# RMS roots at eviction, x loaded first, and two key chunks of layer 1 ahead of the dense feed-forward part, in a two-layer decoder step on one core

## The reference

```
h = RMSNorm(x);  z = h @ w_in              # 2560 columns: B, C, x_conv, x_lru, gate
ya = B * dwconv3(C * x_conv)
yb = RG-LRU(dwconv4(x_lru)) * gelu(gate)   # a scan along the prompt
x += [RMSNorm(ya) | RMSNorm(yb)] @ w_mix_out
k, v = RMSNorm(mem) @ w_k, RMSNorm(mem) @ w_v
x += softmax((RMSNorm(x) @ w_q) k^T / 16) v @ w_o   # samples read k, v from a cache
x += SwiGLU(RMSNorm(x))                    # layer 0: dense, 2816 wide
x += top-2-of-8 MoE SwiGLU(RMSNorm(x))     # layer 1
```

## Time and profile before

| | us |
|---|---|
| runs | 1177.85, 1178.97, 1179.41 |
| median of the runs | 1178.97 |
| profiled execution, device time | 1178.98 |
| its span in the trace | 1177.2 |
| PE busy | 1107.9 (94%) |
| DVE busy | 850.4 (72%) |
| ACT busy | 643.4 (55%) |
| POOL busy | 74.7 (6%) |

### The profile page before, as it was taken

How to read it: one execution, slowest core, us unless ns; L and a number is a source line. 1 busy time by engine, 2 the same in 40 slices (tenths; PEclk the granted TensorE clock), 3 DMA queues, 4 the chain that set the end, 5 groups by cost and what they waited for, 6 DMA issues and landing times.

```text
span 1177.2 us, 21150 instructions
## 1 busy us (share of the span) xinstructions
PE 1107.9 (94%) x8394; PEld 1062.7 (90%) x8394; DVE 850.4 (72%) x1140; ACT 643.4 (55%) x735; POOL 74.7 (6%) x83
## 2 busy tenths in 40 slices
PE   5998999897999999999899988999999999999995
PEld 4998998487999999999799668999999999999995
DVE  4879873257665644778965345989889888989886
ACT  4446451145555433447343136677677767767874
POOL 1012110010000000102211021000000000000000
PEclk8999999998999999999899998999999999999998
DMA  7443546772655654444455783799799879988983
GB/s 275 172 154 134 219 164 260 297 273 84 211 178 178 246 184 143 153 163 158 152 210 215 286 320 116 277 358 362 259 356 359 318 286 354 357 305 304 361 335 128
DMA packets 33846, 284.50 MB, mean 242 GB/s; under 512 B 3888, under 2 KB 3888, under 8 KB 4736
## 3 DMA queue, kind: packets, MB, share of 16 engines
q1 hardware_dynamic: 32832, 278.77, 63.6%
q0 software_dynamic: 960, 4.97, 1.3%
HBM read 278.23 MB, written 5.50 MB: 241 GB/s over the span
## 4 chain that ended last, share of the span: by engine, by line
PE 82%; DVE 9%; ACT 5%; issue 2%; DMA 2%; SPq 0%; DVEq 0%; ACTq 0%
PE ps L1335 23%; PE ps L1336 23%; PE ps L1337 23%; PE ps L1542 2%; PE ps L1576 2%; ACT whi L487 2%; PE ps L1669 2%; DVE rstd L806 2%; DVE wlo L779 1%; PE ps L1562 1%; PE ps L1521 1%; DMA raw<-cache_in_dram 1%; PE ps L1744 1%; DVE hf L821 1%; PE ps L1730 1%
## 5 line engine op out<-in xcount | busy, mean ns | idle before, releaser
L779 DVE TENSOR_TENSOR wlo<-raw,whi 128x1024 fp32r<-128x1024 f32 (+2 forms) x376 | 544.9, 1468 | 158.0 <-ACT whi L487 154.9
L487 ACT ACTIVATE whi<-raw 128x1024 fp32r<-128x1024 f32 (+2 forms) x376 | 462.2, 1239 | 241.6 <-PE ps L1337 203.1
L1335 PE MATMUL ps<-a_hi,whi 128*128 128x264 f32 x1056 | 303.3, 287 | 14.0 <-DVE a_lo L812 8.9
L1336 PE MATMUL ps<-a_lo,whi 128*128 128x264 f32 x1056 | 301.1, 285 | 0.0
L1337 PE MATMUL ps<-a_hi,wlo 128*128 128x264 f32 x1056 | 300.9, 285 | 0.0
L1335 PEld LDWEIGHTS ps<-a_hi,whi 128*128 128x128 f32 x1056 | 200.8, 190 | 16.3 <-issue 10.3
L1336 PEld LDWEIGHTS ps<-a_lo,whi 128*128 128x128 f32 x1056 | 200.8, 190 | 0.1
L1337 PEld LDWEIGHTS ps<-a_hi,wlo 128*128 128x128 f32 x1056 | 199.9, 189 | 0.0
L1335 PE MATMUL ps<-whi,xg_hi 128*128 128x352 f32 x512 | 165.8, 324 | 0.0
L1337 PE MATMUL ps<-whi,xg_lo 128*128 128x352 f32 x512 | 164.9, 322 | 0.0
L1336 PE MATMUL ps<-wlo,xg_hi 128*128 128x352 f32 x512 | 164.3, 321 | 0.0
(11 more groups left out here) (282 smaller groups left out, 1542.5 us busy)
## 6 DMA issues: line engine op xcount, KB each, us to landing
raw<-moe_in_dram SPq DMA_DIRECT2D x100, 1408.0 KB, 7.6
raw<-dense_in_dram SPq DMA_DIRECT2D x60, 1024.0 KB, 4.9
raw<-cache_in_dram SPq DMA_DIRECT2D x24, 1024.0 KB, 6.9
raw<-gu_in_dram SPq DMA_DIRECT2D x22, 1024.0 KB, 4.7
raw<-down_in_dram SPq DMA_DIRECT2D x8, 1408.0 KB, 6.1
spare<-cache_in_dram SPq DMA_DIRECT2D x8, 1024.0 KB, 8.2
v_out<-vt POOLq DMA_DIRECT2D x2, 1024.0 KB, 4.9
k_out<-kt POOLq DMA_DIRECT2D x2, 1024.0 KB, 5.5
```

The costliest lines, as they stand in the source:

```text
L487: act.activation(whi[m % 4][:, 0:w], raw[:, k % RAWS, c:c + w], ACT.Copy).then_inc(hi_done, 1)
L779: dve.tensor_tensor(wlo[m % 4][:, 0:w], raw[:, k % RAWS, c:c + w], whi[m % 4][:, 0:w].bitcast(f32), ALU.subtract).then_inc(lo_done, 1)
L1335: pe.matmul(out, w_hi, m_hi_, start=first, stop=False)
L1336: pe.matmul(out, w_hi, m_lo_, start=False, stop=False)
```

## The change

**Roots at eviction.** Since the root is one number for each column, it may be applied after the product. The operand of the IN, Q, gate/up chunks and of the memory is now x * g without the root: ACT writes `x*g` rounded (`stage_hi`, a copy with a scale), DVE subtracts (`stage_lo`, one instruction for each tile), each tile as soon as its x is ready. The root multiplies at eviction: z, q, k and the down products on DVE by `rstd` or `rstm` as a tensor; the values on ACT, with the root of the memory as a number for each partition (`rcol`, turned by two small matmuls); a gate tile by DVE into `sg` ahead of Silu. The sums for the roots are taken by PE inside the first chunk of the stage that needs them (`folded_sum`, ahead of its last quarter), which for the start and the memory now follow folds by POOL. `norm` and `mem_operand` go. ACT's part of the gate step now reads `sg` in place of PSUM.

**Order of the chunks.** Layer 0 now begins with IN; all its four key chunks (`KX`) stand between V and MIX. Its last two chunks before the gate/up part are the first two key chunks of layer 1 (`K_NEXT`). Layer 1 has IN, V, its other two key chunks, MIX, Q. Nothing stands between MIX and Q or ahead of IN any more.

**Loads.** SP issues the parameters `pk`, the first weight chunk, x in four pieces, two more chunks, half the memory, a chunk, the other half. The first two cache chunks of the attention wait until PE has finished the chunk ahead of MIX.

**The mixer.** The product ya moves from POOL into `lru_input` on DVE. In the V steps both splits of each chunk come as early as they may: `lo(V+2,0)` and `lo(V+2,1)` stand ahead of the scans, and the values are evicted by ACT.

```diff
             sp.dma_start(pk[:], pk_in).then_inc(s_par, 16)
-            load(dense_in[0, 0], 0, 0, DW)
-            sp.dma_start(x[:], x_in).then_inc(s_x, 16)
+            load(dense_in[0], 0, 0, DW)
+            for j in range(4):
+                sp.dma_start(x[:, 2 * j:2 * j + 2], x_in[:, 2 * j:2 * j + 2]).then_inc(s_x[j], 16)
...
+            def stage_hi(name, dst, k):
+                act.activation(dst[:, k], x[:, k], ACT.Copy, scale=stage_gain(name, k)).then_inc(x_h, 1)
...
             act.wait_ge(consts, 4)
             load_table(ACT.Sqrt)
+            hi(0, 0, 0)
+            act.wait_ge(s_par, 16)
             for j in range(4):
-                act.wait_ge(s_mem[j // 2], 16)
-                square(sq[:, 2 * j:2 * j + 2, 0:MEM], memn[:, 2 * j:2 * j + 2])
-            hi(0, 0, 0)
-            hi(0, 0, 1)
-            root("mem", 1.0 / D)
-            norm_hi("m0", lambda k: hf[:, k:k + 2, 0:MEM], m_hi)
-            act.wait_ge(s_x, 16)
+                act.wait_ge(s_x[j], 16)
+                for k in (2 * j, 2 * j + 1):
+                    stage_hi("mix0", a_hi, k)
+                if j == 0:
+                    hi(0, 0, 1)
...
+            def stage_lo(name, src_hi, dst, ks):
+                for k in ks:
+                    dve.wait_ge(x_h, stage_of(name, k + 1))
+                    dve.scalar_tensor_tensor(out=dst[:, k], in0=x[:, k], scalar=stage_gain(name, k),
+                                             in1=src_hi[:, k].bitcast(f32), op0=ALU.mult,
+                                             op1=ALU.subtract).then_inc(x_l, 1)
...
                 def lru_input():
+                    dve.wait_ge(sc_done, l + 1)
+                    dve.tensor_tensor(sc, sc, z[:, ZB:ZB + G], ALU.mult).then_inc(ya_done, 1)
                     dve.wait_ge(gate_a, G * (l + 1))
...
                     chain(dve.tensor_tensor(hs[:, :, SEQ:T], av[:, :, SEQ:T], st_h, ALU.mult))
+                    lo(0, V + 2, 1)
                     chain.wait()
...
+                def scaled_in(j):
+                    return lambda: dve.tensor_tensor(z[:, 2 * j:2 * j + 2, :], banks(IN + j, T), over_pair(rstd), ALU.mult)
...
                 for j in range(4):
-                    step(0, L + MIX + j, lambda: add_x(L + MIX + j, j))
-                keys(3, L + K_C, first=lambda: norm(f"xattn{l}", "g_x", l))
+                    step(0, MIX + j, lambda: add_x(MIX + j, j),
+                         lambda: stage_lo(f"xattn{l}", xq[:, 0], xq[:, 1], (2 * j, 2 * j + 1)))
+                root_reciprocal(f"xattn{l}")
...
                 if l == 0:
-                    norm("ffn0", "g_ffn", 0)
-                    mem_operand(1)
+                    stage_lo("ffn0", a_hi, a_lo, range(KT))
+                    step(0, K_NEXT, lambda: keys(1, 0, K_NEXT))
+                    root_reciprocal("ffn0")
+                    step(0, K_NEXT + 1, lambda: keys(1, 1, K_NEXT + 1))
...
                     def gated(off, j, last=False):
                         k = GU0 + j
+                        dve.wait_ge(pe_done, off * 2 + (2 * k + 1))
+                        dve.tensor_tensor(sg[k % 2][:], ps[:, 2 * (k % 2), 0:T], rstd[:], ALU.mult).then_inc(gate_s, 1)
                         lo(off, k + 2, 0)
...
+            def first_chunk(k, ready, m_h, m_l, w, beside=None):
                 pe.wait_ge(lo_done, 2 * k + 2)
                 if k >= 2:
                     pe.wait_ge(evac, k - 1)
                 for p in range(4):
-                    pe.wait_ge(n_lo, pair_of(name, p + 1))
+                    if beside and p == 3:
+                        beside()
+                    ready(p)
```

More of the change, by code:

```diff
@@ L547, in _, with mem_squares, body, mem_root @@
             for l in range(DEPTH):
[L548 removed]
+                IN, V, KX, MIX, Q, O = places(l)
                 P = pk[:, l, :]
[L551 to L553 removed]
+                root(f"mix{l}", 1.0 / D)
+                def mem_squares(h):
+                    def body():
+                        act.wait_ge(s_mem[h], 16)
+                        for j in (2 * h, 2 * h + 1):
+                            square(sq_m[:, 2 * j:2 * j + 2], memn[:, 2 * j:2 * j + 2])
+                    return body
+                def mem_root():
+                    act.wait_ge(evac, IN + 1)
+                    root("mem", 1.0 / D)
+                    mem_hi(0, range(4, 8))
+                def mem_col():
+                    act.wait_ge(rc_mm, 1)
+                    act.activation(rcol[:], ps[:, 6, 0:4], ACT.Copy).then_inc(rc_cp, 1)
                 def sigmoids(t0):
@@ new lines, in valued, with run @@
+                def valued(j, body=None):
+                    def run():
+                        k = V + j
+                        if body:
+                            body()
+                        act.wait_ge(pe_done, 2 * k + 2)
+                        for t in range(MT):
+                            ins = act.activation(vt[:, t, j * 256:j * 256 + 256], ps[:, 2 * (k % 2) + t, 0:256],
+                                                 ACT.Copy, scale=rcol[:, 2 * t:2 * t + 1])
+                        ins.then_inc(evac, 1)
+                    return run
@@ L849, in _ @@
             lo(0, 0, 0)
+            stage_lo("mix0", a_hi, a_lo, range(0, 2))
             lo(0, 0, 1)
-            dve.wait_ge(n_rt, order["mem"] + 1)
-            chain(dve.reciprocal(rstm[:], rt[:, 0:MEM]))
-            chain.wait()
-            mem_operand(0)
+            stage_lo("mix0", a_hi, a_lo, range(2, KT))
             lo(0, 1, 0)
@@ L1327, in _ @@
                                 hidden_lo(1)
-            norm("fin", "g_fin", 0)
+            root_reciprocal("fin")
+            for k in range(KT):
+                dve.scalar_tensor_tensor(out=hf[:, k], in0=x[:, k], scalar=col(0, "g_fin", k), in1=rstd[:],
+                                         op0=ALU.mult, op1=ALU.mult).then_inc(n_h, 1)
         @block.tensor
@@ L1459, in _ @@
             pe.wait_ge(consts, 4)
-            for j in range(4):
-                sum_pair("mem", sq, j, w=MEM)
             for l in range(DEPTH):
-                L = LAYER0[l]
+                IN, V, KX, MIX, Q, O = places(l)
+                kt = kts[l]
                 by_a = proj(a_hi, a_lo, T)
+                by_q = proj(xq[:, 0], xq[:, 1], T)
                 by_m = proj(m_hi, m_lo, MEM)
@@ L1500, in _ @@
                 gates(2)
                 gates(3)
-                chunks(L + IN + 6, 4, by_a)
-                chunk(0, L + V, values)
-                chunk(0, L + V + 1, values)
-                chunk(0, L + V + 2, beside_v(lambda: group_sum(f"co{l}", xc)))
-                chunk(0, L + V + 3, beside_v(lambda: group_sum(f"lo{l}", ig)))
-                chunk(0, L + K_B, by_m)
-                first_chunk(L + MIX, f"g{l}", a_hi, a_lo, T)
+                chunks(IN + 6, 2, by_a)
+                if l == 0:
+                    pe.wait_ge(gates_act, 2 * G)
+                    pe.wait_ge(rm_done, 1)
+                    for t in range(MT):
+                        last = pe.matmul(ps[:, 6, 2 * t:2 * t + 2], rstm[:, 128 * t:128 * t + 128], ident[:, 0:2],
+                                         start=True, stop=True)
+                    last.then_inc(rc_mm, 1)
@@ L1511, in _ @@
+                chunks(IN + 8, 2, by_a)
+                pe.wait_ge(m_l, KT * (l + 1))
+                for k in range(V, V + 3):
+                    chunk(0, k, values)
+                chunk(0, V + 3, beside_v(lambda: group_sum(f"co{l}", xc)))
+                chunk(0, KX, proj(m_hi, m_lo, MEM, lambda: group_sum(f"lo{l}", ig)))
+                for k in range(KX + 1, MIX):
+                    chunk(0, k, by_m)
+                first_chunk(MIX, group_in(f"g{l}"), a_hi, a_lo, T)
                 for j in range(1, 4):
-                    chunk(0, L + MIX + j, by_a)
```

398 lines of the change are left out of this document (221 added, 177 removed).

## The result

The changed kernel takes 1149.42 us (median of 1148.81 to 1150.01), against 1178.95: a ratio of 0.9751, with an interval of 0.9734 to 0.9768. The forecast was 1143.6 in a range of 1138 to 1152. So the direction and the range held; the gain is 29.5 us where 35.4 were forecast, and the 5.9 us between them are what the experiments had to find.

The account below looks back on a forecast made before the run. PE bounds the kernel, busy 1107.9 of 1177.2 us, so only its idling, half clock behind it and the start can be won. 7.3 + 0.7 + 21.4 + 7.5 - 1.5 = 35.4; 1178.98 - 35.4 = 1143.6 us, range 1138 to 1152.

Parts of the forecast that it names:

- a. The start: Kernel start: first weight chunk lands at 7.6 us, PE begins at 11.9 instead of 19.24; gain 7.3 us (4.1 to 9.0).
- The chain of 4.3 us: Kernel start: ACT's copies and DVE's subtraction between the first weight chunk's landing and PE's first chunk take 4.3 us.
- b. Sums: Norm sums on PE: eight matmuls become three, plus three for the memory and two tiny ones; gain 0.7 us.
- c. Waits: PE's waits for a_lo (8.9), wlo in V (8.0) and at MIX (3.5), and squares (1.0) go: 21.4 us.
- the walk: Step-by-step timing from PE's start of V: third chunk's second split comes at 10.6 us, wanted at 14.
- d. The clock: Four stretches behind PE's long waits ran at 0.51 to 0.56 of full clock; 7.5 us go with the gaps.
- the clock is full elsewhere: Outside the four slow stretches behind long gaps, PE's granted clock was said to be full, 1.00.
- e. What is added: Evictions multiplying by the root cost nothing; added DVE work and tight margins bring 1.5 us of new stalls (0 to 5).
- belong to code whose order stays, and I leave them at what they are: PE's other waits, in attention and MoE, were taken as unchanged.
- DVE did not fall behind: Rival, chance 0.13: layer 0's IN part overruns on DVE, V's splits come late and the gap stays; 1149.3 us, or 1151.1.
- x was not late: Rival, chance 0.07: x's four transfers come serially, last piece in at 21.4 us, delaying the first chunk's end; 1149.7 us.
- The roots did not stall a third chunk: Rival, chance 0.02: the root chain grows from 5.4 to 10.5 us, five stages stall some 3.3 each; 1160 us.
- the gate chunks kept their time: Slower rival, chance 0.02: gate chain exceeds its 8.7 us room, 22 chunks pay; about 1181. Sign: chunks over 5.8 us.

Follow-up runs that it names:

- e6: Changed kernel with the old order of first loads: both memory halves, parameters, first weight chunk, x in four pieces, three more chunks; 1152.48 us.
- e4: Changed kernel with the second split of the third V chunk behind the recurrence again instead of ahead of its scans; 1153.66 us.
- e8: Changed kernel with three V edits undone: ya on POOL, third chunk's second split behind the recurrence, values evicted by DVE; 1160.25 us.
- e2: Changed kernel without key chunks between O and the gate/up part, its root's sum in the first gate/up chunk; roots stay at eviction; 1156.22 us.
- b1: Kernel before the change with an unused 16-byte tile ahead of the large area, moving it by 32 bytes; 1182.58 us.
- e1: Changed kernel with rcol allocated behind the large area, which returns to its old address; 1145.17 us.
- e7: Changed kernel with two edits: rcol behind the large area, and layer 0's first norm sum behind the first chunk; 1145.41 us.
- e10: Changed kernel with rcol behind the area, first sum behind the first chunk, Q's first-chunk splits ahead of tile staging in the third MIX chunk; 1142.48 us.
- e11: Changed kernel once more, unedited; 1149.21 us.
- e3: Changed kernel with the product ya back on POOL, as before the change; 1152.36 us.
- e9: Changed kernel with 32 unused bytes behind rcol, so the large area begins 64 bytes behind its old place; 1145.60 us.

## Why the prediction was right, and where it was off

**a. The start.** The chain of 4.3 us is 4.36. The landing came at 6.41 instead of 7.6, within its bounds: the memory's share was 3.16 (e6) where I had 3.2 and 0.86 of issue; another 2.1 came from something that the sum did not have. The gain is 8.5 instead of 7.3.

**b. Sums.** 3.36 before; now 20.04 - 18.80 = 1.24 us for the first, 1.10 for the memory's and 0.36 for the two small matmuls. Gain 0.66 for 0.7. But the step ended at the matmuls: the fold on POOL ahead of the first sum ended at 18.74, and PE waited 1.33 for it. That is the wait that took the place of the old one.

**c. Waits.** All of the 21.4 us went from where they were. New ones came: 0.34 at the fourth V chunk of layer 1, which the prediction had named as the tight one and priced at 1.6, and 1.27 at Q, which it had not. At Q I had followed the tiles of x, which were in time, and not the second split of the weights, which stands behind their staging on ACT and DVE. V's split came where the walk had it: by this row of DVE it ended 10.4 us after PE's first matmul of V at 79.94, for 10.6 in the walk.

```profile
89.11 1.22 DVE L873 TENSOR_TENSOR wlo<-raw,whi 128x1024 fp32r<-128x1024 f32 x1
```

The cause as told was too narrow. I credited the split's place with 4.7 us; alone it is 1.7 to 2.1 (e4), and the three edits share it (e8). For the gate/up part the prediction named the two key chunks as cover for the copies, and they carry most of the gain (e2). For Q and layer 1 the trace shows the waits gone, and no run undoes the roots there alone.

**d. The clock.** The 7.5 us went with the gaps, as forecast; e8 and e2 bring 3.3 and 1.6 back. But 1.7 of them did not stand behind a wait of some microseconds, as the prediction says. The stretch from 586.00 began 1.43 us behind the end of a gap of 1.74 at MIX. Behind the like gap of 1.75 in layer 0 the same kernel kept its full clock, and b1 kept it behind both:

```profile
136.91:142.00 5.09, 5.09 (x42) 5.09 (x43) 4.05 (x5) 0.00 (x0) 0.28 (x1) 1.00 0.97 344
```

The sentence that the clock is full elsewhere was wrong too: behind the cache's wait and in the last sum the kernel before had 0.58 and 0.67, as shown above. At the start the slow pace lasted 4.54 us instead of 3.56, which the prediction had taken as equal.

**e. What is added.** The eviction with the root costs nothing, 706 ns for 705:

```profile
L1075 DVE TENSOR_TENSOR z<-ps,rstd 128x528 f32<-128x528 f32 x20 | 14.1, 706 | 4.2 <-PE ps L1443 4.1
...
L921 DVE SCALAR_TENSOR_TENSOR m_lo<-memn,pk,m_hi 128x256 fp32r<-128x256 f32 x16 | 9.6, 655 | 0.1
```

Against this the prediction had set the Trainium skill's table ("VectorE: DVE Perf Modes", the perf-mode tier table), by which a copy from PSUM may run up to twice as fast as an operation on two tensors. The same page limits float32 operands in PSUM to the single rate (section "Why PSUM operands drop a tier"), so by the whole page neither form gains here, and the trace agrees, 706 for 705 ns.

The memory's subtractions took 655 ns instead of 489, but the IN part of layer 0 kept its cover: no wait in V of that layer. The new stalls are 1.33 + 1.27 + 0.34 = 2.9 us, where I had 1.5 and a range of 0 to 5, and all but the 0.34 came where I had looked for none.

Together: 8.5 + 0.7 + 21.4 + 7.5 - 2.9 = 35.2, against the 35.56 of the landmarks. That the sum of these terms came out within 0.2 us of the forecast is in part luck: the start gave 1.2 more than forecast, and the new stalls took 1.4 more.

**The step that was mis-sized** is the sentence that waits of attention and MoE "belong to code whose order stays, and I leave them at what they are". They were priced at no change, and these stretches cost 2.98 + 2.43 + 1.05 = 6.46 us.

- The MoE's part is shown to be the address of the area (e1, b1). In all profiled executions the MoE took 427.30 to 428.24 us with the area at its old place (the kernel before, e1, e7, e10), and 430.67 to 432.08 with the area 32 bytes on (the changed kernel, e11, b1, e2 to e6, e8). Two profiles of the same kernel, the changed one, differ by 1.35.
- The cache's longer wait, 1.74 us, mostly repeats, but its cause is open. The 1.2 us of clock behind it do not follow the wait. From there to the next product the changed kernel took 6.34 us and the kernel before 5.14. But e3 took 4.86 behind a wait of 6.09, e9 6.02 behind 7.74, and the kernel before, in layer 0, 6.23 behind 4.61.
- The last microsecond is the half clock at the end, which lasted longer in this execution: 1.1 us by the rows above. When the unedited kernel was profiled again (e11), the same stretch to the end took 1148.7 - 1130.72 = 18.0. Of all profiles only e1 and e9 show 18.9 to 19.0 as well, and the eleven others 17.9 to 18.0, so that microsecond is not the change's.

**The rivals.** DVE did not fall behind: from PE's first chunk to V in layer 0 it was busy 61.46 of 69.17 us. x was not late: its four pieces were all in before PE wanted them. The roots did not stall a third chunk, and the gate chunks kept their time: 863 matmuls in 104.00 us, as before, and no wait of PE in them. The total came to lie where two of the rivals had put it, 1149.3 and 1149.7, but by neither of their mechanisms.

## What to carry to other kernels

Take a landmark that both kernels pass with the same work done, and subtract: it separates the terms that were forecast from those that were not, here 35.6 us from -6.5. Profile the same kernel again before a microsecond of such a difference is given a cause. A gap that has several causes can't be given to the one whose shift happens to be long enough; undo each alone and all together, since the last microsecond of a gap may also cost the clock. And look at where a new tile is allocated: put small tiles behind the large ones, so that no operand that runs in a bound stage changes its address.
